# Moving one of four channel tiles of a depthwise convolution from VectorE to ScalarE and the Pool engine

## The reference

```python
u = h @ w_in                                    # h: 256 tokens x 1024
q, k, v, ga, gb = split(u, 512 columns each)
attn = dilated_attention(q, k, v, slopes)       # 8 heads of 64
# conformer_conv
g = ga * sigmoid(gb)
y = depthwise_causal_conv(g, conv_w, width=31) + conv_b      # each of 512 channels by itself
conv = silu(layer_norm(y, ln_g, ln_b))          # over the 512 channels
mix = concat([attn, conv]) @ w_out
x = x + gt1 * mix
# then a router and 32 experts, two for each token
```

## Time and profile before

| | |
|---|---|
| median of 3 runs | 1291.69 us (1289.37 to 1295.06) |
| the profiled execution | 1294.49 us |
| its span, first to last instruction | 1292.6 us |
| TensorE's mean granted clock | 0.973 of full |

### The profile page before, as it was taken

One profiled execution on the slowest core, in us unless ns is written; L12 is line 12 of the kernel. 1 busy time (PEld: TensorE's weight loads), 2 busy tenths in 40 slices (PEclk: granted clock), 3 DMA queues, 4 the chain that ended last, 5 costly groups with the idle time before them and its releaser, 6 DMA issues.

```text
span 1292.6 us, 14532 instructions
## 1 busy us (share of the span) xinstructions
PE 1226.7 (95%) x5854; PEld 667.8 (52%) x5854; DVE 422.8 (33%) x1013; ACT 286.6 (22%) x642; POOL 20.1 (2%) x29
## 2 busy tenths in 40 slices
PE   4999999989999999999899798899999999999997
PEld 2446446654574447667687467544444444444442
DVE  1211008961341000691429833122222222222213
ACT  0000018860240001570400333111111111111102
POOL 0000000000001000120000000000000000000000
PEclk9899999999989999999899888999999999999999
DMA  9921524013344213456533656488999999999994
GB/s 342 389 98 65 195 85 176 2 53 143 107 155 132 88 65 116 116 169 217 195 131 130 260 202 254 190 331 345 427 428 427 427 429 429 429 427 427 428 425 177
DMA packets 81901, 311.28 MB, mean 241 GB/s; under 512 B 17969, under 2 KB 18812, under 8 KB 69050
## 3 DMA queue, kind: packets, MB, share of 16 engines
q1 hardware_dynamic: 78384, 309.56, 61.2%
q10 hardware_dynamic: 3386, 0.86, 0.3%
q0 software_dynamic: 80, 0.15, 0.0%
HBM read 309.39 MB, written 1.17 MB: 240 GB/s over the span
## 4 chain that ended last, share of the span: by engine, by line
PE 70%; DMA 17%; DVE 9%; ACT 2%; SPq 1%; issue 1%; DVEq 0%; ACTq 0%
PE ps L625 18%; DMA ring<-in_w_exp_up 15%; PE ps L920 12%; PE ps L733 9%; PE ps L621 5%; PE ps L950 4%; DVE G L1580 4%; PE ps L566 3%; PE ps L683 3%; PE ps L697 2%; PE ps L670 2%; PE ps L887 2%; PE ps L899 2%; PE ps L782 2%; PE ps L577 2%; DMA ring<-in_w_ada 2%
## 5 line engine op out<-in xcount | busy, mean ns | idle before, releaser
L625 PE MATMUL ps<-U,ring 128*128 128x512 f32 (+1 forms) x800 | 267.2, 495 | 5.0 <-ACT U L1138 3.6
L920 PE MATMUL ps<-ring,prob 128*64 128x512 f32 x976 | 217.6, 593 | 5.3 <-DMA ring<-in_w_exp_up 4.3
L625 PEld LDWEIGHTS ps<-U,ring 128*128 128x128 f32 x800 | 153.3, 192 | 112.3 <-issue 99.9
L920 PEld LDWEIGHTS ps<-ring,prob 128*64 128x64 f32 x976 | 71.2, 137 | 143.8 <-issue 131.1
L950 PE MATMUL ps<-ring,prob 128*64 128x512 f32 x512 | 113.4, 595 | 0.0
L733 PE MATMUL ps<-U,ring 128*128 128x256 f32 (+1 forms) x384 | 110.9, 451 | 0.0
L733 PEld LDWEIGHTS ps<-U,ring 128*128 128x128 f32 x384 | 72.7, 190 | 37.5 <-issue 31.0
L1715 DVE TENSOR_TENSOR prob<-ps,prob 128x512 f32<-128x512 f32 x16 | 17.3, 1079 | 202.2 <-PE ps L920 202.2
L621 PE MATMUL ps<-ring,U 128*128 128x512 f32 (+1 forms) x224 | 83.1, 531 | 0.0
L950 PEld LDWEIGHTS ps<-ring,prob 128*64 128x64 f32 x512 | 35.4, 137 | 66.6 <-issue 66.6
L887 PEld LDWEIGHTS ps<-bias,U 128*128 128x128 f32 x512 | 60.0, 196 | 15.1 <-issue 15.1
(11 more groups left out here) (238 smaller groups left out, 1019.8 us busy)
## 6 DMA issues: line engine op xcount, KB each, us to landing
ring<-in_w_exp_gate SPq DMA_DIRECT2D x30, 2048.0 KB, 15.1
ring<-in_w_exp_down SPq DMA_DIRECT2D x30, 2048.0 KB, 12.2
ring<-in_w_exp_up SPq DMA_DIRECT2D x29, 2048.0 KB, 17.3
ring<-in_w_ada SPq DMA_DIRECT2D x12, 2048.0 KB, 14.9
ring<-in_w_mod SPq DMA_DIRECT2D x12, 2048.0 KB, 8.2
ring<-in_b_w_in SPq DMA_DIRECT2D x8, 2048.0 KB, 8.4
ring<-in_a_w_in SPq DMA_DIRECT2D x5, 2048.0 KB, 19.8
ring<-in_w_in SPq DMA_DIRECT2D x5, 2048.0 KB, 8.3
```

The costliest lines, as they stand in the source:

```text
L625: last = mm(ps[:, b, 0:wid], w[:, col:col + P], src[:, k, 0:wid], start=(k == 0), stop=(k == KT - 1))
L920: last = mm(ps[x * CAP:(x + 1) * CAP, 2 + i, :], xg[:, k, x * CAP:(x + 1) * CAP], chunk(n, 2 * i + x)[0][:, k, :], start=(k == 0), stop=(k ...
```

## The change

VectorE keeps three of the four tiles. For the fourth, ScalarE multiplies: the first tap and the channel bias go straight into `convo`, and each of the other 30 products goes into one of six buffers `prods`. The Pool engine adds the products to `convo`, one after the other, each behind the one before. ScalarE's products stand in its list behind its q and k evacuations, four behind each (three behind the last), and product k waits until add k-6 is done.

```diff
+        PB = 6
+        prods = Q[:, 2048:2048 + PB * S].rearrange("p (b t) -> p b t", b=PB)
...
+        prod_ok, prod_used = sem("prod_ok"), sem("prod_used")
...
+            for k in range(1, CONV_W):
+                pool.wait_ge(prod_ok, k + 1)
+                if k >= 2:
+                    pool.wait_ge(prod_used, k - 1)
+                pool.tensor_tensor(convo[:, 3, :], convo[:, 3, :], prods[:, k % PB, :], ALU.add
+                                   ).then_inc(prod_used if k < CONV_W - 1 else conv_ok, 1)
...
                         how(kind, m, i % 4).then_inc(tk[stage, "act"], 1)
+                        if kind in "qk" and stage == "c_in":
+                            taken = sum(j[4] == "act" for j in jobs[:i]) - 4
+                            conv_products(4 * taken, min(4 * taken + 4, CONV_W))
...
+            def conv_products(first, last):
+
+                act.wait_ge(tk["c_in", "dve"], 4)
+                for k in range(first, last):
+                    taps = conv_taps[:, 3, k:k + 1]
+                    if k == 0:
+                        a(convo[:, 3, :], glu[:, 3, 0:S], ACT.Identity, scale=taps, bias=vc("conv_b_2", 3)
+                          ).then_inc(prod_ok, 1)
+                        continue
+                    if k > PB:
+                        act.wait_ge(prod_used, k - PB)
+                    a(prods[:, k % PB, :], glu[:, 3, k:k + S], ACT.Copy, scale=taps).then_inc(prod_ok, 1)
...
-            for j in range(4):
+            for j in range(3):
                 step(v.tensor_scalar(convo[:, j, :], glu[:, j, 0:S], conv_taps[:, j, 0:1], vc("conv_b_2", j),
                                      ALU.mult, ALU.add))
             for k in range(1, CONV_W):
-                for j in range(4):
-                    dve.wait_ge(dve_step, base + 4 * (k - 1) + j + 1)
+                for j in range(3):
+                    dve.wait_ge(dve_step, base + 3 * (k - 1) + j + 1)
```

## The result

| | before | changed |
|---|---|---|
| median | 1292.95 us (4 runs, 1289.37 to 1295.06) | 1306.32 us (4 runs, 1301.75 to 1312.37) |
| ratio, with its 95% interval | | 1.0101 (1.0072 to 1.0130) |
| the profiled execution | 1294.49 us | 1301.75 us |
| its span | 1292.6 us | 1299.8 us |

The change makes the kernel 1% slower, 13.4 us by the medians. The prediction was 1293.0 us in a range of 1285.5 to 1299.5. The four runs of the changed kernel lie in two pairs (1301.75 and 1302.27, 1310.36 and 1312.37), and its median falls between them; the profile is of the quickest.

A forecast was written before the change was run, and what follows sets the result against it. VectorE's convolution was taken as the bound, with TensorE waiting only 4.09 us for it. Relief of 12.2 us against 13.5 us of blocked turns left it 1.3 us later: 1291.7 + 1.3 = 1293.0 us, range 1285.5 to 1299.5.

The forecast's parts named there:

- The bound and the ceiling: VectorE's convolution ends the stretch; TensorE waits for it only 4.09 us, the most a shorter convolution gives at unchanged clock.
- rival (a): Convolution: VectorE and Pool do not disturb each other; 4.1 to 7.5 us gained, part from TensorE's clock; chance 0.21.
- a gain there reaches the end whole: Behind the convolution: later weight loads follow released buffers, so the expert stage moves as a whole.
- Removed from VectorE: Convolution: one first tap and 30 multiply-adds leave VectorE, 12.2 us; only the first 4.1 us are worth time.
- added on ScalarE: Between q and k evacuations: 31 multiplications of about 0.51 us, costing nothing while Pool hands back buffers.
- Added on Pool: Fourth tile: 30 additions of 0.57 to 0.64 us, a step 0.8 up to 1.0 us, ending near 705, hidden.
- What the adds do to VectorE: Convolution: Pool additions block two-input multiply-adds at 0.45 us each, so it ends at 721.5, 1.3 us later.
- the price of a turn: VectorE's loss for each Pool addition in the convolution: 0.37, 0.43, at most 0.61 us; taken as 0.45.
- the sum's term of 13.5 us: VectorE's convolution: 30 blocked turns of 0.45 us each, added to its end at 707.95.
- turn-taking: Convolution: VectorE's multiply-adds and Pool's additions alternate, each addition costing VectorE about 0.45 us.
- The cover on ScalarE: Product k waits for add k-6, evacuations and TensorE behind it; Pool may take 1.5 us for each add.
- the case at +13.8 us: Convolution: Pool gets no turn, ScalarE stops at product 7, TensorE stands until 708; about 1305.5 us, chance 0.06.

The follow-up runs named there:

- products_only: Changed kernel without the Pool additions, ScalarE still writing all 31 products: 1289.5 us, ratio 0.9962 to the kernel before.
- psum_three: Changed kernel with VectorE's three running sums in PSUM until the last tap: 1289.67 us, ratio 0.9950 to the kernel before.
- adds_alone: Kernel before, all four tiles on VectorE, plus 30 chained Pool additions on scratch data: 1312.17 us, ratio 1.0117 to before.
- one_gap: Changed kernel with one VectorE memset of scratch between tap 5 and tap 6: 1296.35 us, ratio 1.0015 to the kernel before.
- the repeat: The changed kernel run once more, nothing altered: 1311.92 us, ratio 1.0120 to the kernel before.

## Why the prediction was wrong

**The bound and the ceiling** were right. The convolution carried the path, and only its first microseconds were worth anything: the idle time of 4.1 us went in every kernel where VectorE finished early. The clock came on top, as rival (a) had allowed: folding in 2.77 us instead of 5.21. A relief of 12.2 us gives 7.3 us in the stretch. That a gain there reaches the end whole is not borne out: products_only and psum_three gain 4 us by the medians, 4.9 and 6.5 by the ratio, and in both profiles what lies behind the stretch is 3.6 to 4.0 us longer than before.

**Removed from VectorE and added on ScalarE** were right: 35.7 us for 90 multiply-adds against a reckoned 35.6, and 31 products that cost nothing (products_only).

**Added on Pool** was too low in size: 0.72 us for 256 columns, 0.86 from one to the next, where I took 0.57 to 0.64 and 0.8. It did not matter.

**What the adds do to VectorE** is the step that failed. That the two exclude each other because of two SBUF inputs was right (psum_three), and the price of a turn was right where turns are taken: 0.48 us measured in adds_alone and one_gap, 0.45 predicted. But in the changed kernel no turns were taken: the sum's term of 13.5 us on VectorE came out as nothing (35.71 us for 90 multiply-adds), and in its place stand one Pool addition of 32.93 us and TensorE's stop of 17.91 us. What failed was to carry turn-taking over to the changed kernel. In the earlier trace rows Pool's addition at 534.26 begins with the first TENSOR_SCALAR of a pair, and the additions at 550.10 and 562.49 begin inside pairs that end soon. None begins inside a long stream of VectorE. I counted an addition let in after one instruction as evidence that a Pool addition always gets in; it was evidence for a queue of two. The diff shows the order: Pool's first product cannot exist before ScalarE's first q evacuation. It comes 3.4 us into VectorE's stream, and Pool pays for that with 33 us.

The Trainium skill ("SBUF — State Buffer", Who interferes with whom) says that a two-input VectorE instruction contends with a GpSimd one that reads SBUF, and that the first to start keeps the interface for the whole instruction. The runs agree on the contention: 46.3 us for an addition beside two SBUF inputs, 0.74 at most beside one. They differ on the length. It is not one instruction of 0.48 us for which Pool waits, but the unbroken rest of the stream, about 82 multiply-adds in the changed kernel. Where turns are taken, the runs agree on the length too: in one_gap the multiply-add that waits lasts 0.948 us, its own 0.48 and the rest of one addition.

**The cover on ScalarE.** I named the wait for add k-6, the evacuations behind it, and TensorE behind them, and priced the case at +13.8 us and 1305.5 us. The measured stretch is +12.9, the repeat +13.3, the median 1306.3. The place was right. That the price fits so well is partly luck: the stop and the slow restart cost 19.7 us where 16.5 were reckoned, and the idle time before the first transposes and the folding at full clock, which the price left out, gave 3.8 us back. The chance of 0.06 rested on those additions beside pairs and was too low, and the range was drawn to leave this case out.

**What stays open.** Why a stream keeps Pool out and Pool does not keep VectorE out is not settled. VectorE starts a multiply-add every 0.396 us and each lasts 0.475 to 0.49, so the next begins before the last ends, while two chained Pool additions leave about 0.14 us between them (one_gap). That alone does not explain it: at 694.44 in one_gap the next multiply-add also began 0.07 us before the last had ended, and Pool got in. Pool was let in when it came during the first or second multiply-add behind a memset or a delayed one, and shut out during the fifth or the ninth; where the border lies, and why, no run varied.

## What to carry to other kernels

Before work is moved to the Pool engine beside VectorE, count VectorE's SBUF inputs: with two, the engines exclude each other, and a Pool instruction that arrives in the middle of an unbroken stream may wait for its end. One input is no guarantee: the TENSOR_SCALAR of the earlier trace rows and of adds_alone has a single SBUF tensor and was slowed as well. In this kernel, with the running sum in PSUM, both ran at full speed. And where a third engine waits for Pool with a few buffers, price the case that Pool does not run at all, since what stands behind that wait is what the kernel pays with.

## What the runs showed of the hardware

- An addition of 0.72 us on Pool took 32.9 us beside 90 VectorE multiply-adds with both tensors in SBUF, and 46.3 us beside 120, when it came during the ninth and the fifth of them; VectorE was not slowed (0.396 us a step). When Pool came first, VectorE lost 0.48 us for each addition and Pool 0.06 (0.787 us at the median in adds_alone).
- A single VectorE memset of 0.27 us let Pool in, and the other 29 additions took 0.754 us at most, also the one behind an idle time of 0.51 us of Pool (one_gap).
- The first taps of adds_alone, TENSOR_SCALAR with one SBUF tensor, took 0.88 us at the median beside Pool instead of 0.41.
- With the sum in PSUM the same multiply-add steps at 0.393 us, and Pool's additions take 0.72 to 0.74 us beside it.
